# Second feed-forward product of chunks 0 to 6 as one level of Strassen's method on two token tiles, its weight sums formed by GpSimd

## What is computed

```python
D_MODEL = 2048
D_FF = 4 * D_MODEL
    h = rmsnorm(x, g_ffn_pre)
    z = jnp.square(jax.nn.relu(h @ w_ff1))
    return x + rmsnorm(z @ w_ff2, g_ffn_post)
```

## Time and profile before

| | us |
|---|---|
| median of three runs | 1960.72 (1958.95 to 1961.06) |
| the profiled execution | 1961.18 |
| its span, first to last instruction | 1959.6 |

### The profile page before, as it was taken

How to read it: one execution, slowest core, us unless ns; L and a number is a source line. 1 busy time by engine, 2 the same in 40 slices (tenths; PEclk the granted TensorE clock), 3 DMA queues, 4 the chain that set the end, 5 groups by cost and what they waited for, 6 DMA issues and landing times.

```text
span 1959.6 us, 26732 instructions
## 1 busy us (share of the span) xinstructions
PE 1932.0 (99%) x10594; PEld 1783.1 (91%) x10594; DVE 856.0 (44%) x1119; ACT 661.5 (34%) x932; POOL 190.2 (10%) x243
## 2 busy tenths in 40 slices
PE   8999999999999999999999999999999999999997
PEld 8998999989999998888989899899898898998996
DVE  5654444433333334456444444434334344444446
ACT  4344434332333333335323223233233232232332
POOL 1462233310010101001000000000000000000000
PEclk9999999999999999999999999999999999999999
DMA  7457888844444436424343434444443444434442
GB/s 203 123 140 170 190 201 146 205 130 128 126 127 130 126 123 225 161 76 140 124 125 123 135 118 129 133 126 129 130 124 125 128 129 129 128 125 126 127 129 86
DMA packets 210321, 269.45 MB, mean 138 GB/s; under 512 B 15329, under 2 KB 138433, under 8 KB 209312
## 3 DMA queue, kind: packets, MB, share of 16 engines
q1 hardware_dynamic: 194912, 235.98, 41.6%
q0 software_dynamic: 15296, 31.90, 5.4%
HBM read 260.69 MB, written 7.08 MB: 137 GB/s over the span
## 4 chain that ended last, share of the span: by engine, by line
PE 94%; DVE 2%; DMA 2%; POOL 1%; ACT 1%; issue 0%; DVEq 0%; SPq 0%; POOLq 0%; ACTq 0%
PE ps L493 18%; PE ps L495 18%; PE ps L494 18%; PE ps L520 12%; PE ps L519 11%; PE ps L521 11%; DMA w_raw<-in_w_in_dram 2%; PE ps L670 1%; PE ps L736 0%; PE ps L687 0%; POOL win_s L2104 0%; DVE w_lo L1454 0%; PE ps L658 0%; PE ps L741 0%; DVE z_gain L2049 0%
## 5 line engine op out<-in xcount | busy, mean ns | idle before, releaser
L1454 DVE TENSOR_TENSOR w_lo<-w_raw,w_hi 128x1024 fp32r<-128x1024 f32 x426 | 532.5, 1252 | 818.6 <-ACT w_hi L1004 815.4
L1004 ACT CAST w_hi<-w_raw 128x1024 fp32r<-128x1024 f32 x426 | 446.6, 1050 | 864.9 <-PE ps L495 439.4
L493 PE MATMUL ps<-ht_hi,w_hi 128*128 128x384 f32 x2000 | 676.0, 338 | 7.4 <-DVE ht_lo L1499 3.4
L495 PE MATMUL ps<-ht_hi,w_lo 128*128 128x384 f32 x2000 | 669.7, 335 | 0.0
L494 PE MATMUL ps<-ht_lo,w_hi 128*128 128x384 f32 x2000 | 669.5, 335 | 0.0
L493 PEld LDWEIGHTS ps<-ht_hi,w_hi 128*128 128x128 f32 x2000 | 376.6, 188 | 9.5 <-issue 5.4
L494 PEld LDWEIGHTS ps<-ht_lo,w_hi 128*128 128x128 f32 x2000 | 376.6, 188 | 1.3 <-issue 0.9
L495 PEld LDWEIGHTS ps<-ht_hi,w_lo 128*128 128x128 f32 x2000 | 376.3, 188 | 0.0
L520 PE MATMUL ps<-w_lo,z_hi 128*128 128x512 f32 x762 | 300.2, 394 | 0.0
L519 PE MATMUL ps<-w_hi,z_hi 128*128 128x512 f32 x762 | 298.7, 392 | 0.0
L521 PE MATMUL ps<-w_hi,z_lo 128*128 128x512 f32 x762 | 295.7, 388 | 0.0
(11 more groups left out here) (274 smaller groups left out, 1308.2 us busy)
## 6 DMA issues: line engine op xcount, KB each, us to landing
w_raw<-in_w_ff_dram SPq DMA_DIRECT2D x256, 512.0 KB, 3.7
w_raw<-in_w_in_dram SPq DMA_DIRECT2D x130, 512.0 KB, 7.5
w_raw<-in_w_out_dram SPq DMA_DIRECT2D x32, 512.0 KB, 4.2
kc<-in_cache_k_dram POOLq DMA_DIRECT2D x8, 1024.0 KB, 12.3
vc<-in_cache_v_dram POOLq DMA_DIRECT2D x8, 1024.0 KB, 12.0
w_raw<-in_w_attn_up_dram SPq DMA_DIRECT2D x16, 512.0 KB, 3.7
bias_s<-ncs_dram POOLq DMA_DIRECT2D x64, 48.0 KB, 6.8
out_dram<-z_gain SPq DMA_DIRECT2D x6, 512.0 KB, 2.7
```

Of the source, the lines that this page charges most:

```text
L493: pe.matmul(out, wh[:, k, cols], x_hi[:, kk, :], start=(kk == 0), stop=False)
L495: last = pe.matmul(out, wl[:, k, cols], x_hi[:, kk, :], start=False, stop=(kk == k_last))
L1004: nc.scalar.copy(w_hi[:, u % RING, :], w_raw[:, u % RAWS, :]).then_inc(hi_ready, 1)
L1454: nc.vector.tensor_tensor(w_lo[:, u % RING, :], w_raw[:, u % RAWS, :], f32(w_hi[:, u % RING, :]), ALU.subtract).then_inc(lo_ready, 1)
```

## The change

**Products.** In chunks 0 to 6 the product with `w_ff2` is done in two pairs of column groups (1024 columns each). For token tiles 0 and 1, the eight block products of a 2 x 2 by 2 x 2 block scheme (token tiles 0 and 1, even and odd hidden tiles, two column groups) become seven, Q1 to Q7, of sums of blocks. Tile 2 takes plain products against the blocks that are there (C31, and E from T1 and T4). The right-hand sides of a pair are 14 converted units, made from 8 loaded ones: B11, B22, B21 and the sums T3, T1, T2, T4, each in two halves ("_0", "_1") of the hidden rows. B12 is only used in sums. TensorE takes 6 matmuls of 512 columns for every product that a unit has in `PRODUCTS` (one or two).

**Weight sums.** GpSimd forms T3 = B12 + B22, T1 = B11 + B12, T2 = T3 + B11, T4 = T2 + B21 in place, in the raw slots, 128 x 1024 each: eight for a pair, 16 for a chunk. Each waits for the sum before it, and T3 and T4 also for the `w_lo` of the unit that they overwrite. ScalarE and VectorE then convert a sum as they do a loaded unit, so a chunk has 44 conversions and not 32 (`CONVS`). A chunk still loads 32 units.

**Row sums.** Of each pr of `z`, GpSimd forms five sums of 128 x 128 blocks in four instructions (`row_sums`), which ScalarE and VectorE split in high and low (`sums_hi`, `sums_lo`). The ReLU now writes `z_sq`, which is squared in place.

**Raw slots, sums, residual.** From chunk 0's second half on there are 12 raw slots, six of them over `xres`; the residual is written to DRAM (`xres_dram`) and loaded back (`x_back`) in the last chunk. Nine PSUM sums for a pair are added onto `acc` in SBUF, 18 for a chunk where there were 12. In the last chunk, whose own product is plain, GpSimd first combines the 18 sums in 16 instructions of 128 x 512; VectorE waits for them (`comb`) ahead of its part of the second half.

```diff
+U_X = U_FFN + 16
+XRAWS = 12
+CONVS = 44
+C_LAST = U_FFN + CONVS * (NCHUNK - 1)
+assert U_X % RAWS == 0
+ROLES = ("B11_0", "B22_0", "B12_0", "B21_0", "B11_1", "B22_1", "B12_1", "B21_1")
+RHS = ("B11_0", "B22_0", "B21_0", "T3_0", "B11_1", "B22_1", "B21_1", "T3_1",
+       "T1_0", "T2_0", "T1_1", "T2_1", "T4_0", "T4_1")
+HOME = {"T3": "B22", "T1": "B12", "T2": "B11", "T4": "B21"}
+SUMS = ("T3_0", "T1_0", "T2_0", "T3_1", "T1_1", "T2_1", "T4_0", "T4_1")
+FREED = {"B22": "T2", "B12": "T1", "B11": "T4", "B21": "T4"}
+A11, A31, A22, A12, A32, S1, S5, S2, S3, S4 = range(10)
+PRODUCTS = {"B11": (("Q1", A11), ("C31", A31)), "B22": (("Q3", S4),), "B21": (("Q2", A12), ("C31", A32)),
+            "T3": (("Q7", S3),), "T1": (("Q5", S1), ("E", S5)), "T2": (("Q6", S2),), "T4": (("Q4", A22), ("E", A32))}
+OPENED = {"Q1": 0, "C31": 0, "Q3": 1, "Q2": 2, "Q7": 3, "Q5": 8, "E": 8, "Q6": 9, "Q4": 12}
+CLOSED = {"Q1": 4, "C31": 6, "Q3": 5, "Q2": 6, "Q7": 7, "Q5": 10, "E": 13, "Q6": 11, "Q4": 13}
+EVICTED = ("Q1", "Q3", "Q2", "C31", "Q7", "Q5", "Q6", "E", "Q4")
...
+            def freed(c0, r):
+                if r < 0:
+                    c0, r = c0 - 1, r + 32
+                base = U_FFN + CONVS * c0
+                if r < 16 or c0 == NCHUNK - 1:
+                    return base + r + 1
+                pair, m = divmod(r - 16, 8)
+                kind, half = ROLES[m].split("_")
+                return base + 16 + 14 * pair + RHS.index(FREED[kind] + "_" + half) + 1
+            def load_x(c0, r, lap, src, k, w):
+                dst, landed, _ = unit_at(c0, r)
+                j = 32 * c0 - 16 + r
+                if j < RAWS:
+                    sp.wait_ge(lo_ready, U_X - RAWS + j + 1)
+                elif j < XRAWS:
+                    sp.wait_ge(x_spilled, 16 * TT)
+                    sp.wait_ge(hn_ready, TT)
+                else:
+                    sp.wait_ge(lo_ready, freed(c0, r - XRAWS) + lap * (3 * CONVS))
+                sp.dma_start(dst.rearrange("p (k w) -> p k w", w=w), src).then_inc(landed, 16)
...
+            def product(cb, more, idx, pair):
+                kind, half = RHS[idx].split("_")
+                n = cb + 16 + 14 * pair + idx
+                slot = unit(n, more)
+                wh = w_hi[:, slot, :].rearrange("p (k w) -> p k w", w=512)
+                wl = w_lo[:, slot, :].rearrange("p (k w) -> p k w", w=512)
+                for q, blk in PRODUCTS[kind]:
+                    out = ps[:, Q_BANK[pair][q], :]
+                    for k in range(2):
+                        pr = 2 * int(half) + k
+                        begins = OPENED[q] == idx and k == 0
+                        ends = CLOSED[q] == idx and k == 1
+                        pe.matmul(out, zb_hi[:, pr, blk, :], wh[:, k, :], start=begins, stop=False)
+                        pe.matmul(out, zb_hi[:, pr, blk, :], wl[:, k, :], start=False, stop=False)
+                        last = pe.matmul(out, zb_lo[:, pr, blk, :], wh[:, k, :], start=False, stop=ends)
+                last.then_inc(unit_used, 1)
...
+                for idx in range(14):
+                    if idx == 0:
+                        pe.wait_ge(za_lo, c * 4 + (2 if c0 else 3))
+                    elif idx == 1:
+                        pe.wait_ge(zs_lo, c * 4 + (2 if c0 else 3))
+                    elif idx == 3:
+                        pe.wait_ge(relu_ready, c * 4 + 3)
+                    elif idx == 4:
+                        pe.wait_ge(za_lo, c * 4 + 4)
+                    elif idx == 5:
+                        pe.wait_ge(zs_lo, c * 4 + 4)
+                    elif idx == 8:
                         pe.wait_ge(relu_ready, c * 4 + 4)
-                    elif cg >= 2:
-                        pe.wait_ge(o_added, c * 12 + 3 * (cg - 1))
-                    for tiles in ((0,), (1,), (2,)) if is_last and cg == 3 else ((0, 1, 2),):
-                        for q in range(4):
-                            if cg == 0:
-                                pe.wait_ge(z_lo_ready, c * 4 + (q + 1) if later(c) else max(3, q + 1))
-                            down(n + 16 + 4 * cg + q, more, banks, 2 * q, z_hi, z_lo,
-                                 CHUNK // P - 1, o_psum, tiles)
-            chunk(U_FFN, 0, 0)
+                    elif idx == 12:
+                        pe.wait_ge(o_added, c * 18 + 1)
+                    product(cb, more, idx, 0)
+                for idx in range(14):
+                    if idx in (0, 1, 2, 3, 8, 9, 12):
+                        pe.wait_ge(o_added, c * 18 + {0: 4, 1: 4, 2: 5, 3: 6, 8: 8, 9: 9, 12: 10}[idx])
+                    product(cb, more, idx, 1)
...
+                act.wait_ge(unit_used, cb + k - RING + 1 + lap * (3 * CONVS))
+                nc.scalar.copy(w_hi[:, (cb + k) % RING, :], raw).then_inc(hi_ready, 1)
...
+            def rectified(c0, lap, c, pr):
+                b = 2 - 2 * (pr % 2)
+                act.wait_ge(unit_used, U_FFN + CONVS * c0 + 4 * pr + 4 + lap * (3 * CONVS))
+                if c0 or pr == 3:
+                    act.wait_ge(za_lo, c * 4 + pr)
+                    act.wait_ge(s_done, c * 4 + (0 if c0 == NCHUNK - 1 else pr))
+                nc.scalar.activation(z_sq[:, :, :], ps[:, b:b + 2, 0:T], ACT.Relu).then_inc(relu_ready, 1)
+            def sums_hi(c, pr, nth):
+                act.wait_ge(s_done, c * 4 + nth + 1)
+                nc.scalar.copy(zb_hi[:, pr, 5:10, :], s_f[:, :, :]).then_inc(zs_hi, 1)
...
+            def blocks_lo(c, pr, nth, src):
+                dve.wait_ge(za_hi, c * 4 + nth + 1)
+                nc.vector.tensor_tensor(zb_lo[:, pr, 0:5, :].rearrange("p b c -> p (b c)"), src,
+                                        f32(zb_hi[:, pr, 0:5, :]).rearrange("p b c -> p (b c)"),
+                                        ALU.subtract).then_inc(za_lo, 1)
+            def sums_lo(c, pr, nth):
+                dve.wait_ge(zs_hi, c * 4 + nth + 1)
+                nc.vector.tensor_tensor(zb_lo[:, pr, 5:10, :], s_f[:, :, :], f32(zb_hi[:, pr, 5:10, :]),
+                                        ALU.subtract).then_inc(zs_lo, 1)
...
+            def evict(c0, pair, q):
+                bank = ps[:, Q_BANK[pair][q], :]
+                if c0 == 0:
+                    nc.vector.tensor_copy(acc(pair, q), bank).then_inc(o_added, 1)
+                else:
+                    nc.vector.tensor_tensor(acc(pair, q), bank, acc(pair, q), ALU.add).then_inc(o_added, 1)
...
+                if not is_last:
+                    for k in range(16, CONVS + 1):
+                        if k < CONVS:
+                            convert(c0, lap, k + 2)
+                        if k == 17:
+                            sums_lo(c, 3, 3)
+                        for pair in range(2):
+                            done = k - 1 - 16 - 14 * pair
+                            for q in EVICTED:
+                                if CLOSED[q] == done:
+                                    dve.wait_ge(unit_used, cb + 16 + 14 * pair + done + 1 + lap * (3 * CONVS))
+                                    evict(c0, pair, q)
+                    return
...
+            def row_sums(c0, c, nth, z, steps):
+                tiles = z.rearrange("p e (t c) -> p e t c", c=P)
+                if c0 == 0 and nth in (1, 2):
+                    pool.wait_ge(zf_done, TT)
+                else:
+                    pool.wait_ge(sq_ready, c * 4 + (3 if c0 == 0 and nth == 0 else nth + 1))
+                if c0 or nth:
+                    pool.wait_ge(zs_lo, c * 4 + nth)
+                nc.gpsimd.tensor_tensor(s_f[:, 0:2, :], tiles[:, 0, 0:3:2, :], tiles[:, 1, 0:3:2, :],
+                                        ALU.subtract).then_inc(s_step, 1)
+                nc.gpsimd.tensor_tensor(s_f[:, 3, :], tiles[:, 0, 0, :], tiles[:, 0, 1, :], ALU.subtract)
+                pool.wait_ge(s_step, steps + 1)
+                nc.gpsimd.tensor_tensor(s_f[:, 2, :], tiles[:, 0, 1, :], s_f[:, 0, :], ALU.subtract).then_inc(s_step, 1)
+                pool.wait_ge(s_step, steps + 2)
+                nc.gpsimd.tensor_tensor(s_f[:, 4, :], tiles[:, 1, 1, :], s_f[:, 2, :], ALU.subtract).then_inc(s_done, 1)
+            def weight_sum(c0, lap, pair, name):
+                kind, half = name.split("_")
+                base = U_FFN + CONVS * c0 + 16 + 14 * pair
+                u0 = 16 + 8 * pair
+                def raw(role):
+                    return unit_at(c0, u0 + ROLES.index(role + "_" + half))
+                def converted(rhs):
+                    pool.wait_ge(lo_ready, base + RHS.index(rhs + "_" + half) + 1 + lap * (3 * CONVS))
+                def summed(other):
+                    pool.wait_ge(sum_ready, 16 * c0 + 8 * pair + SUMS.index(other + "_" + half) + 1 + lap * 48)
+                if kind == "T3":
+                    converted("B22")
+                    pool.wait_ge(raw("B12")[1], raw("B12")[2] + lap * (96 // XRAWS * 16))
+                    a, b = raw("B12")[0], raw("B22")[0]
+                elif kind == "T1":
+                    summed("T3")
```

(83 more changed lines are left out.)

349 lines of the change are left out of this document (230 added, 119 removed).

## The result

| | us |
|---|---|
| before, beside the changed kernel | 1960.89 (1958.95 to 1961.17) |
| after, median of four runs | 2054.43 (2053.66 to 2055.53) |
| ratio | 1.0479, 95% interval 1.0466 to 1.0492 |
| profiled execution, after | 2053.86, its span 2052.3 |

A forecast was written before the change was run, and what follows sets the result against it. TensorE, busy 99%, was taken as the bound. Fewer matmuls save 38.4 us, waits in seven `w_ff2` halves add 7 x 19.7: 1961.2 becomes 2061, median 2060; range 2012 to 2098.

The forecast's parts named there:

- Part 3: `w_ff2` halves: GpSimd sums and VectorE subtractions exclude each other; TensorE waits 19.7 us a chunk, half 80.1 us.
- Its exception: VectorE additions from PSUM to SBUF, such as evictions at 0.64 us each, take no turns with GpSimd sums.
- Rival 1: Sums and subtractions don't exclude each other, or GpSimd gives way: faster, 1930 us; chance 0.04.
- Part 2: Cost of a GpSimd weight sum of 1024 columns: 2.40 us, between 2.06 and 2.45.
- The schedule of Part 3: Both pairs of a `w_ff2` half followed step by step: pair 0 ends at 41.6 us, pair 1 at 80.1.
- the 1 us behind the last ReLU: Start of the `w_ff2` half: `w_lo` of B21_0 late behind the last ReLU, about 1 us a chunk, were sums free.
- The sum: Total for the profiled execution: 1961.2 - 38.4 + 7 x 19.7 = 2061 us; median 2060.
- Part 4: Further casts, row sums, evictions, DMA, residual and the 16 final combinations: counted at nothing.
- The upper bound from DMA: Bursts of weight loads at 7.5 us each: the last load 10 to 20 us late.
- Rival 2: About as before, 1955 to 1965 us: waits of 5.5 us a chunk, needing sums at some 1.5 us; chance 0.02.
- Rival 3: TensorE's granted clock falls to 0.91 in seven `w_ff2` halves: 42 us more, 2102; chance 0.06, including slow load bursts.
- Rival 4: The change doesn't do what it says; a third pass for C31 and E would return 12 matmuls; chance under 0.01.

The follow-up runs named there:

- the fills: Changed kernel with each GpSimd weight sum replaced by one 64-column sum and 15 zero fills of 64 columns; 1934.44 us.
- the third experiment: Kernel before, with 112 GpSimd sums on a spare tile that nobody waits for, 16 in each of seven chunks; 1963.13 us, ratio 1.0014.
- the 768 columns show: Changed kernel with GpSimd's weight sums over 768 of 1024 columns, the rest left out; 1998.18 us.
- the run without the long wait: Changed kernel with the split of the last row sums two units later in ScalarE's and VectorE's order; 2051.49 us, ratio 1.0467.

## Why the prediction was right, point by point

**The mechanism.** Part 3's claim, that a weight sum and a subtraction exclude each other for their whole length and take turns, is shown: by the changed kernel's timelines, by the fills (nearly all reads gone, `w_lo` at 1.25 us and 120 us back), and by the sums for nobody in the kernel before (2.86 us a subtraction). Its exception holds too, as the evictions kept 0.68 us; its 0.64 for them is a misreading of a row of two, of no weight in the sum. The Trainium skill (SBUF — State Buffer, § Who interferes with whom) says that a VectorE instruction with two SBUF inputs contends with a GpSimd instruction that reads SBUF, and not with one that only writes it. The runs agree on both halves, 2.86 against 1.23 us and 1.25 beside the fills. Rival 1 leant on another page of the Trainium skill (Advanced Engine Details and Errata, § VectorE Performance Modes, Mode Summary), whose note names two-port instructions alone. By that note the time would have been 1930 us; the measured 2054 decides against it.

**The price of a sum, Part 2.** 2.40 us taken, 2.40 measured where nothing is beside it. The extrapolation from the 768 columns of the earlier trace rows by the slope held to the hundredth for a sum of two tiles; of one tile with itself it is 1.90, as the third experiment shows. The estimate of 2.25 us from the Trainium skill's figure (GPSIMD Engine Reference, § 3.1 Elementwise) is 6% short of the 2.40 measured. A sum shorter by 0.15 us, 15 times in each of seven chunks, would have put the forecast some 16 us lower.

**The schedule of Part 3**, from the start of the half, in us:

| | predicted | measured |
|---|---|---|
| unit 4 starts | 13.6 | 13.0 |
| unit 10 starts, pair 0 | 32.05 | 31.1 |
| pair 1, unit 10 starts | 70.5 | 69.2 |
| half | 80.1 | 79.0 |

The waits, by TensorE's weight loads in pair 0; one row of pair 1 follows, the last before its unit 10:

```profile
1250.95 0.18 PEld L1066 LDWEIGHTS ps<-w_hi,zb_hi 128*128 128x128 f32 x1 [1.52 <-DVE w_lo L2197]
1258.59 0.19 PEld L1066 LDWEIGHTS ps<-w_hi,zb_hi 128*128 128x128 f32 x1 [3.65 <-DVE w_lo L2197]
1270.02 0.19 PEld L1066 LDWEIGHTS ps<-w_hi,zb_hi 128*128 128x128 f32 x1 [1.67 <-DVE w_lo L2197]
1273.36 0.19 PEld L1066 LDWEIGHTS ps<-w_hi,zb_hi 128*128 128x128 f32 x1 [0.73 <-DVE w_lo L2197]
1276.70 0.19 PEld L1066 LDWEIGHTS ps<-w_hi,zb_hi 128*128 128x128 f32 x1 [2.12 <-DVE w_lo L2197]
...
1314.73 0.19 PEld L1066 LDWEIGHTS ps<-w_hi,zb_hi 128*128 128x128 f32 x1 [2.09 <-DVE w_lo L2197]
```

They stand before units 2, 4, 8, 9 and 10. Predicted were 4, 7, 8 and 10. Unit 2's was in the prediction only as the 1 us behind the last ReLU; it is 1.5. Unit 7 has no wait because the units ahead of it ran at a lower clock and TensorE came to it later, as the point on the rivals tells. In the chunk at 1685.30 the clock stayed at 1.00, and there unit 7 waits as predicted:

```profile
1706.22 0.19 PEld L1066 LDWEIGHTS ps<-w_hi,zb_hi 128*128 128x128 f32 x1 [1.38 <-DVE w_lo L2197]
```

**The term that was mis-sized** is the half, 1.0 us too long, 7 us for seven chunks. The first sum of pair 1 starts at 40.8 and not 41.5, and from there to unit 10 it takes 28.4 and not 29.0 us: turns and waits between the eight sums are 8.0 us and not 8.5, the last conversion and start 1.1 and not 1.3. The count of sums on the chain was right, as the 768 columns show.

**The sum.** Predicted were 99 us more. The span grew by 92.7: the first chunk's 14.4, five typical ones' 12.8 to 13.0 each, one of 15.0 at the border between the loop's laps, 94.0 together, less 1.4 us that were won before chunk 0's last ReLU (2.5 us in the run without the long wait, so this part scatters); behind the last ReLU 76.18 us stand against 76.15, so the 16 combinations and the residual's way back cost nothing. The border's extra 2 us were not foreseen; without them the miss would be 2 us larger, so that much of the closeness is luck.

**Part 4, the edits at nothing.** In the half at 1245.57 TensorE's only waits are for `w_lo`, none for ScalarE, a bank or a DMA. Loads land later, but nobody notices (part 6 of the page, beside the earlier trace rows):

```profile
w_raw<-in_w_ff_dram SPq DMA_DIRECT2D x136, 512.0 KB, 5.0
x_raw<-in_w_ff_dram SPq DMA_DIRECT2D x120, 512.0 KB, 6.2
```

The upper bound from DMA was not reached, and nothing of it shows.

**The rivals.** Rival 1's 1930 is near what the kernel takes without the exclusion (1934 with the fills, 1936 without sums, both with less GpSimd time than it assumed), so its price was about right and its condition false. Rival 2's about as before needed sums of 1.5 us; at 1.84 the time is 1998, so it was not near (the step from there to 1.5 is not measured). Rival 3, the clock, happened in small. TensorE's row after its longest wait, the stretches behind it:

```profile
1258.59 0.50 PE L1066 MATMUL ps<-w_hi,zb_hi 128*128 128x512 f32 x1 [3.22 <-DVE w_lo L2197]
...
1258.60:1260.00 1.40, 1.40 (x5) 1.18 (x6) 1.40 (x2) 0.00 (x0) 0.25 (x1) 0.80 0.00 0
1260.00:1262.00 2.00, 2.00 (x6) 1.52 (x6) 0.81 (x1) 0.00 (x0) 2.00 (x1) 0.50 0.00 0
1262.00:1264.00 2.00, 2.00 (x9) 1.59 (x8) 0.00 (x0) 0.77 (x1) 1.92 (x2) 0.79 0.00 0
```

For some 3 us the granted clock is at 0.50, 1.2 GHz, and a matmul takes 0.43 us in place of 0.23. But the `w_lo` of the units behind is late then anyway, on the chain of sums, and the lost time comes out of the waits for them. Two things show it: the half at 1685.30, with the same wait of 3.65 us and the clock at 1.00, takes 79.05 us and this one 79.06; and the run without this wait has halves as long. The 42 us of rival 3 took the mean clock for all halves, which was not to be had from so few places. Rival 4: TensorE's count of instructions rules it out.
